# One core, an adaptive-norm block and a sparse-attention block in float32: the set-up of the first block is reordered

## The reference

```python
mod = (c @ w_ada[l] + b_ada[l])[:, None, :]            # c: (1, 1024), w_ada: (1024, 6144)
sh_m, sc_m, gt_m, sh_f, sc_f, gt_f = jnp.split(mod, 6, axis=-1)
h = rms_norm(x, g_pre_mix[l]) * (1.0 + sc_m) + sh_m
z = h @ w_in[l]
u, f, q, k, v = jnp.split(z, splits, axis=-1)
y_ssm = s5_mixer(u, lam_re, lam_im, log_dt, b_re, b_im, c_re, c_im, d_skip, w_glu)
...
x = x + gt_m * rms_norm(y, g_post_mix[l])
h = rms_norm(x, g_pre_ffn[l]) * (1.0 + sc_f) + sh_f
...
```

## Time and profile before

| | us |
|---|---|
| three runs | 3245.16, 3250.99, 3251.94 |
| median | 3250.99 |
| span of the profiled execution | 3246.9 |
| median less that span | 4.1 |
| PE busy in the span | 3019.4 (93%) |
| DVE, ACT, POOL busy in the span | 2163.2, 1251.2, 273.8 |
| first modulation matmul of the chain | 31.32 |
| tap matmuls begin | 114.04 |

### The profile page before, as it was taken

One profiled execution on the slowest core, in us unless ns is written; L12 is line 12 of the kernel. 1 busy time (PEld: TensorE's weight loads), 2 busy tenths in 40 slices (PEclk: granted clock), 3 DMA queues, 4 the chain that ended last, 5 costly groups with the idle time before them and its releaser, 6 DMA issues.

```text
span 3246.9 us, 36670 instructions
## 1 busy us (share of the span) xinstructions
PE 3019.4 (93%) x13313; PEld 2339.1 (72%) x13313; DVE 2163.2 (67%) x3880; ACT 1251.2 (39%) x2183; POOL 273.8 (8%) x287
## 2 busy tenths in 40 slices
PE   6999889799999999999999998986898799999997
PEld 2576566678888888788888875764446678888886
DVE  5562923899988667766665683997542876666567
ACT  1121333544444554433334443234543343333443
POOL 4200210110000000200000000113330010000000
PEclk9899899899999999999999997987999999999999
DMA  8323013324444874354448731111003335444864
GB/s 284 117 51 69 1 34 104 110 97 155 161 160 158 285 258 137 120 166 155 154 158 308 217 124 57 39 27 37 1 1 111 118 114 162 158 156 156 308 208 149
DMA packets 350920, 436.97 MB, mean 135 GB/s; under 512 B 35281, under 2 KB 197065, under 8 KB 350614
## 3 DMA queue, kind: packets, MB, share of 16 engines
q1 hardware_dynamic: 340954, 428.48, 40.1%
q10 hardware_dynamic: 9788, 6.16, 0.6%
HBM read 317.78 MB, written 116.50 MB: 134 GB/s over the span
## 4 chain that ended last, share of the span: by engine, by line
PE 80%; DVE 13%; ACT 3%; issue 1%; ACTq 1%; DMA 1%; POOL 0%; DVEq 0%
PE psum L1876 34%; PE psum L1333 19%; PE psum L991 4%; PE psum L3635 3%; DVE count_junk L3060 3%; PE psum L3606 3%; PE psum L1867 3%; PE psum L2680 3%; PE psum L2858 2%; PE psum L2758 1%; PE psum L2838 1%; PE psum L390 1%; DVE p L3124 1%; PE psum L2848 1%; PE psum L358 1%
## 5 line engine op out<-in xcount | busy, mean ns | idle before, releaser
L1333 PE MATMUL psum<-far_op,far_op 128*128 128x512 f32 x2772 | 629.4, 389 | 0.0
L1333 PEld LDWEIGHTS psum<-far_op,far_op 128*128 128x128 f32 x2772 | 520.2, 188 | 107.9
L1876 PE MATMUL psum<-x_b,w_near 128*128 128x512 f32 x1440 | 348.1, 391 | 3.9 <-DVE w_near L1505 3.9
L1876 PE MATMUL psum<-x_t,w_near 128*128 128x512 f32 x1440 | 337.1, 389 | 0.7 <-ACT psum L1614 0.6
L1876 PE MATMUL psum<-x_t,w_far 128*128 128x512 f32 x1440 | 336.3, 389 | 0.0
L1876 PEld LDWEIGHTS psum<-x_b,w_near 128*128 128x128 f32 x1440 | 272.0, 189 | 61.2 <-issue 4.3
L1876 PEld LDWEIGHTS psum<-x_t,w_near 128*128 128x128 f32 x1440 | 270.1, 188 | 58.0 <-ACT psum L1614 2.0
L1876 PEld LDWEIGHTS psum<-x_t,w_far 128*128 128x128 f32 x1440 | 270.2, 188 | 56.4 <-ACT u_keep L1626 0.4
L1104 DVE TENSOR_TENSOR far_op<-far_a,far_op 128x512 fp32r<-128x512 f32 x231 | 160.6, 695 | 176.2 <-ACT far_op L1097 174.7
L1097 ACT CAST far_op<-far_a 128x512 fp32r<-128x512 f32 x231 | 143.9, 623 | 315.9 <-PE psum L1333 307.7
L1876 PE MATMUL psum<-x_b,w_far 128*128 128x512 f32 x720 | 178.9, 399 | 10.1 <-DVE val_row L1746 10.1
(11 more groups left out here) (484 smaller groups left out, 5145.0 us busy)
## 6 DMA issues: line engine op xcount, KB each, us to landing
far_a<-row_ops SPq DMA_DIRECT2D x231, 256.0 KB, 2.9
row_ops<-hidden SPq DMA_DIRECT2D x99, 512.0 KB, 5.1
raw<-in_ffn_w SPq DMA_DIRECT2D x88, 512.0 KB, 4.5
col_sums<-hidden SPq DMA_DIRECT2D x66, 512.0 KB, 5.7
far_b<-col_sums SPq DMA_DIRECT2D x132, 256.0 KB, 3.2
ada_w<-in_w_ada SPq DMA_DIRECT2D x12, 2048.0 KB
raw<-in_w_up SPq DMA_DIRECT2D x44, 512.0 KB, 3.9
hidden<-in_ffn_w SPq DMA_DIRECT2D x44, 512.0 KB
```

Source lines behind the costliest of these rows:

```text
L1333: ins = t.matmul(bank(b + n), l[slot][:, rows], r[slot][:], start=(fresh and i == 0 and m == 0), stop=(i == FH - 1 and m == 2), skip_group ...
L1876: ins = t.matmul(bank(b), at[:, l, cols], x[:, k, r], start=(start and k == 0 and m == 0), stop=(k == 3 and m == 2), skip_group_check=not ...
```

## The change

Placement: `c_plain` and `e_tmp` move within the memory, `ada_b` becomes one tile of two rows of 1024, and two tiles are new: `bias_cols` [128, 4, 8] and `b_rows` [48, 2048]. Semaphore counts follow. The core of the diff, by engine.

SP queue:

```diff
             cols = slice(HALF * j, HALF * (j + 1))
-            sp.dma_start(ada_w[j % 3][:], w_ada[:, :, cols]).then_inc(ada_in[j % 3], 16)
-            sp.dma_start(ada_b[j % 3][:], a["b_ada"][:, cols]).then_inc(ada_in[j % 3], 16)
+            for k in range(0, KD, 4):
+                sp.dma_start(ada_w[j % 3][:, k:k + 4], w_ada[:, k:k + 4, cols]).then_inc(ada_in[j % 3], 16)
...
         sp.wait_ge(vec_used, 1)
-        sp.wait_ge(carry_ready, 2)
```

ACT queue, after the loads of lam_re, lam_im and log_dt:

```diff
+        act.dma_start(dskip_rows[:], a["d_skip"][0].rearrange("(g c) -> g c", c=GC)).then_inc(ssm_in, 16)
         for i, name in enumerate(("b_re", "b_im")):
             for d in range(2):
-                act.dma_start(b_raw[:, i, d, :, :],
-                              a[name][0, d].rearrange("(q e) p c -> (e p) q c", e=2)).then_inc(ssm_in, 16)
+                at_row = PAIRS * (2 * i + d)
+                act.dma_start(b_rows[at_row:at_row + PAIRS, :],
+                              a[name][0, d].rearrange("(q e) p c -> q (e p c)", e=2)).then_inc(b_c_in, 16)
         for i, name in enumerate(("c_re", "c_im")):
             for twice in range(2):
                 act.dma_start(c_rows[:, i, :, twice, :],
-                              a[name][0].rearrange("(b g) c p -> (g c) b p", b=3)).then_inc(ssm_in, 16)
-        act.dma_start(dskip_rows[:], a["d_skip"][0].rearrange("(g c) -> g c", c=GC)).then_inc(ssm_in, 16)
+                              a[name][0].rearrange("(b g) c p -> (g c) b p", b=3)).then_inc(b_c_in, 16)
...
+        for i, part in enumerate((0, 3)):
+            at_row = 2 * wide + 2 * KD * i
+            act.dma_start(vec_rows[1][at_row:at_row + 2 * KD, :],
+                          a["b_ada"][0, D * part:D * (part + 2)].rearrange("(k p) -> k p", p=P)).then_inc(vec_in, 16)
+        for i, part in enumerate((2, 5)):
+            act.dma_start(ada_b[:, i, :], a["b_ada"][:, D * part:D * (part + 1)]).then_inc(bc_in, 16)
...
-        act.wait_ge(mod_ready, 1)
         for n in range(2):
             split(n)
+        act.wait_ge(mod_ready, 1)
```

DVE (the waits on `ssm_in` go from 16 * 12 to 16 * 4):

```diff
+        def input_columns():
+
+            flat = b_raw[:].rearrange("p r d q c -> p (r d q) c")
+            for i in range(2):
+                dve.wait_ge(b_turned, i + 2)
+                steps.add(v.tensor_copy(flat[:, :, GC // 2 * i:GC // 2 * (i + 1)],
+                                        bank(6 + i, GC // 2 * 4 * PAIRS).rearrange("p (c m) -> p m c", c=GC // 2)))
+            steps.settle()
...
         steps.settle()
+        dve.sem_inc(lam_used, 1)
...
             steps.add(v.tensor_tensor(col(9), col(9), col(9), ALU.mult))
+        dve.wait_ge(c_turned, 2)
+        output_columns()
+        input_columns()
         dve.wait_ge(prm_trig, 2)
...
-            if kind % 2 and half == 1:
-                steps.add(v.scalar_tensor_tensor(mod_cols[:, kind, :], stat_c[:, 0:KD], 1.0,
-                                                 norm_cols[:, kind // 2, :], ALU.add, ALU.mult))
+            if half == 1:
+                sums = stat_c[:, 0:KD] if kind % 2 else mod_cols[:, kind, :]
+                steps.add(v.tensor_tensor(sums, sums, bias_cols[:, kind, :], ALU.add))
                 steps.settle()
-
-        dve.wait_ge(bc_in, 48)
+                if kind % 2:
+                    steps.add(v.scalar_tensor_tensor(mod_cols[:, kind, :], sums, 1.0, norm_cols[:, kind // 2, :], ALU.add, ALU.mult))
+                    steps.settle()
...
+        modulation_used(0)
+        vector_columns()
         for k in range(1, CH):
-            modulation_used(k - 1)
             complex_step(lam_b_at(k), lam_b_at(k - 1), 13, 14)
+            if k == 3:
+                dve.wait_ge(bc_in, 16 * 5)
+            modulation_used(k)
...
             elif n == 5:
+                dve.wait_ge(carry_ready, 2)
                 turns(v, steps, 0)
```

PE:

```diff
             pe.wait_ge(ada_in[j % 3], 32 * (j // 3 + 1))
-            if j == 2:
-                pe.wait_ge(vec_used, 1)
-            elif j >= 4:
+            if j >= 4:
                 pe.wait_ge(ada_used, j - 3)
+            part, half = j // 2, j % 2
+            rows = part in (2, 5)
             for k in range(KD):
-                t.matmul(bank(j % 4), c_bcast[:, k, :], ada_w[j % 3][:, k, :], start=(k == 0), stop=False)
-            t.matmul(bank(j % 4), ones_row[:], ada_b[j % 3][:], start=False, stop=True).then_inc(ada_mm, 1)
+                t_last = t.matmul(bank(j % 4), c_bcast[:, k, :], ada_w[j % 3][:, k, :], start=(k == 0), stop=(k == KD - 1 and not rows))
+            if rows:
+                pe.wait_ge(bc_in, 16 * 5)
+                t_last = t.matmul(bank(j % 4), ones_row[:], ada_b[:, part // 3, HALF * half:HALF * (half + 1)], start=False, stop=True)
+            t_last.then_inc(ada_mm, 1)
...
         pe.wait_ge(ident_in, 16)
-        pe.wait_ge(vec_in, 16 * 6)
...
-        pe.wait_ge(ssm_in, 16 * 12)
+        pe.wait_ge(ssm_in, 16 * 4)
...
         ins.then_inc(lam_turned, 1)
+        pe.wait_ge(b_c_in, 16 * 8)
+        lines = 4 * PAIRS
+        for i in range(2):
+            if i:
+                pe.wait_ge(lam_used, 2)
+            for n in range(GC // 2):
+                ins = t.transpose(bank(6 + i, lines, lines * n), b_rows[:].rearrange("r (m c) -> r c m", c=GC)[:, GC // 2 * i + n, :],
+                                  ident[0:lines, 0:lines])
+            ins.then_inc(b_turned, 1)
...
         pe.wait_ge(c_spread, 2)
-        for j in range(N_ADA - 2):
+        for j in range(2):
+            modulation(j)
+        pe.wait_ge(vec_in, 16 * 8)
+        pe.wait_ge(c_ready, 2)
+        t.transpose(bank(4, 2 * wide + 2 * KD), vec_rows[0][0:2 * wide + 2 * KD, :], ident[0:2 * wide + 2 * KD, 0:2 * wide + 2 * KD])
+        t.transpose(bank(5, 2 * wide + 4 * KD), vec_rows[1][0:2 * wide + 4 * KD, :],
+                    ident[0:2 * wide + 4 * KD, 0:2 * wide + 4 * KD]).then_inc(rows_turned, 1)
+        for j in range(2, N_ADA - 2):
             modulation(j)
```

More of the change, by code:

```diff
@@ L106, in body @@
     log_dt_rows = const("log_dt_rows", [GROUPS, 2])
+    bias_cols = const("bias_cols", [P, 4, KD])
     x_rows = place("x_rows", [P, NT, D], GR)
@@ L111, in body @@
     junk2 = place("junk2", [P, P], GR + 39 * KB + 512)
-    c_plain = place("c_plain", [P, 2, PAIRS, GC], GR + 36 * KB)
+    c_plain = place("c_plain", [P, 2, PAIRS, GC], RR + 19 * KB)
     ada_w = [place(f"ada_w{i}", [P, KD, HALF], at) for i, at in enumerate((XR, XR + 16 * KB, GR + 64 * KB))]
     c_bcast = place("c_bcast", [P, KD, P], RR + 40 * KB)
-    ada_b = [place(f"ada_b{i}", [1, HALF], at) for i, at in enumerate((XR + 56 * KB, XR + 58 * KB, GR + 80 * KB))]
+    ada_b = place("ada_b", [1, 2, D], GR + 80 * KB)
+    b_rows = place("b_rows", [4 * PAIRS, P * GC], XR + 32 * KB)
     vec_rows = [place(f"vec_rows{i}", [P, P], RR + 512 * i) for i in range(2)]
@@ L121, in body @@
     w_tmp = place("w_tmp", [P, 2, 4, PAIRS, GC], RR + 34 * KB)
-    e_tmp = place("e_tmp", [P, 4, PAIRS, GC], RR + 4 * KB)
+    e_tmp = place("e_tmp", [P, 4, PAIRS, GC], RR + 16 * KB)
     c_pad = place("c_pad", [P, 2, PAIRS, 2, GC], XR + 60 * KB)
@@ L153, in body @@
     lam_turned, c_turned, c_ready = sem("lam_turned"), sem("c_turned"), sem("c_ready")
+    b_turned, lam_used = lam_turned, dt_spread
     prm_angle, prm_trig, prm_lam = (sem(n) for n in ("prm_angle", "prm_trig", "prm_lam"))
     lam_b_ready, win_turned, win_ready, k_mm, k_ready = (sem(n) for n in ("lam_b_ready", "win_turned", "win_ready", "k_mm", "k_ready"))
-    carry_ready, k_shift_in, k_low, k_in_dram, toep_in = (sem(n) for n in ("carry_ready", "k_shift_in", "k_low", "k_in_dram", "toep_in"))
+    carry_ready, k_shift_in, k_in_dram, toep_in = (sem(n) for n in ("carry_ready", "k_shift_in", "k_in_dram", "toep_in"))
+    b_c_in, K_SHIFT_0 = k_shift_in, 16 * 8
     x_sq, x_var, x_std, x_scaled, x_turned, h_ready = (sem(n) for n in ("x_sq", "x_var", "x_std", "x_scaled", "x_turned", "h_ready"))
@@ L743, in body @@
     out_first, out_raw, out_s31, out_s42, wt_in, OUT_0 = ada_in[0], ada_in[1], x_in, toep_in, ada_in[2], 16 * NT
-    out_t13, T13_0, out_t42, T42_0 = ssm_in, 16 * 12, k_in_dram, 16 * 15
+    out_t13, T13_0, out_t42, T42_0 = ssm_in, 16 * 4, k_in_dram, 16 * 15
     s_sums, S_SUMS_0, wt_sums, WT_SUMS_0 = y_mm, 6, x_turned, 2 * KD
-    ops_in, OPS_IN_0 = (small_in, ident_in, bc_in, vec_in, k_shift_in, fw_in), (16, 16, 48, 96, 16, 80)
+    ops_in, OPS_IN_0 = (small_in, ident_in, bc_in, vec_in, k_shift_in, fw_in), (16, 16, 80, 128, K_SHIFT_0 + 16, 80)
     f_hi, f_lo, f_mm, F_0 = win_hi, z_ready, win_mm, len(win_units)
@@ L3337, in _ @@
         v.tensor_copy(c_bcast[:], c_cols[:].unsqueeze(2).to_broadcast([P, KD, P])).then_inc(c_spread, 1)
-        dve.wait_ge(ssm_in, 16 * 12)
+        dve.wait_ge(ssm_in, 16 * 4)
         v.tensor_copy(lam_rows[:, 2, :].rearrange("r (e p) -> r e p", e=2),
                       log_dt_rows[:].unsqueeze(2).to_broadcast([GROUPS, 2, STATE])).then_inc(dt_spread, 1)
[L3342 to L3351, removed]
-        steps.add(v.memset(c_pad[:], 0.0))
```

(65 more changed lines are left out.)

2 lines of the change are left out of this document (1 added, 1 removed).

## The result

The changed kernel takes 3228.6 us (median of 4 runs, 3215.8 to 3230.7), the kernel before 3251.15 (median of 4, 3245.2 to 3251.9). The ratio of the two is 0.9929, with a 95% interval of 0.9913 to 0.9945: 22.5 us less, where 20.4 was forecast. The profiled executions show less, spans of 3246.9 and 3228.6, 18.3 us. The time of the profiled execution after is 3230.67, so 2.1 us lie around the span; the 4.1 taken in the prediction held some 2 us by which that execution was simply faster than the median.

What follows compares the result with a forecast made beforehand. PE's chain, started by the ACT queue's loads, was taken as the bound. 13.3 + 8.4 - 0.6 - 0.7 = 20.4 us off 3250.99 gave 3230.6; the range was 3223 to 3242.

Steps and rivals of the forecast that it cites:

- the 4.1 taken in the prediction: Whole kernel: the median was taken to stand 4.1 us above the profiled execution's span.
- PE and not DVE is the chain: Set-up: PE sets the end; DVE's lam_b_ready at 89.5, 4 us ahead of PE at 93.6.
- PE's start: Set-up: PE begins modulation 0 at 18.0 (bounds 15.9 and 20.2) instead of 31.32, 13.3 us earlier.
- the landing of b and c: Set-up loads: landed at 11.3, or 14.8 with c at 88 ns a run; 12.6 us taken.
- Rival 2: Set-up loads: c lands at 20 to 22, PE starts about 26; gain 12.4, time 3239; chance 0.12.
- The bias: PE, first ten modulations: eight lose their bias pair of 1.05 each, 8.4 us less.
- Vector rows: PE between modulations 1 and 2: two transposes of the vector rows added, cost 0.6 us.
- late slice: PE ahead of modulation 2: wait for w_ada's third slice, 0 to 1.6 us, 0.7 taken.
- DVE: DVE's set-up chain: waits for c at 17.1, step 0 at 25.9, lam_b_ready at 89.5; additions cost nothing.
- 4: Set-up loads: c takes 2.1 at 22 ns per run, PE starts at 14.5; gain 23.9, time 3227; chance 0.09.
- 5: Set-up loads: b's 12-row loads run on one DMA engine, landing at 44; gain -11, time 3262; chance 0.04.
- 1: Set-up: DVE becomes the bound, price 4.6, gain 15.8, time 3235; chance 0.14.

Runs made afterwards that it cites:

- e4: Changed kernel with w_ada's first load issued only when b and c have landed; 3231.7 us, median of 5 runs.
- e8: Changed kernel with a bias pair in all 12 modulations (for eight, the row added is not the bias); 3247.0 us, ratio to before 0.9991.
- e5: Changed kernel with w_ada's slices 1 and 2 issued only when b and c have landed, slice 0 at once; 3234.0 us, median of 10 runs.
- e7: Changed kernel with b loaded in runs of 64 B straight into its layout, its transposes and copies gone; 3239.1 us, ratio to before 0.9966.
- e1: Changed kernel with each slice of w_ada in one load instead of two; 3231.1 us, ratio to before 0.9941.
- e2: Changed kernel with each slice of w_ada in four loads instead of two; 3232.6 us, ratio to before 0.9942.
- e12_before_hold: Kernel before with w_ada's slices 1 and 2 issued only when all state-space parameters have landed; 3232.0 us, 1 run.

## Why the prediction was right, and where it was not

- *PE and not DVE is the chain, and a us ahead of the taps is a us at the end.* Right: chain and margin are as read, 2.2 us where 4 were expected.
- *PE's start, 13.3 us earlier.* Wrong by 8.8: it was 4.5. The failed term is the landing of b and c, 11.3 to 14.8 forecast, 23.4 measured, and it failed in two places. b was priced by its bytes, 2.2 us, to be through by 4.8; its last row ended at 12.0. Alone, in e4, it was through at 7.1, so the long rows cost more than their bytes without w_ada too, and the step from there to 12.0 is w_ada beside them; why the rows are so slow stays open. c was taken near the average pace of 51 ns. That average mixed two paces of before: 93 ns a run beside w_ada, and 10 ns once it was through (2,152 runs from 22.2 to 23.6 us). c now had w_ada beside it to the end and went at 101 ns, over even the 88 of the upper bound. Rival 2 (landing at 20 to 22, PE at 26) is what happened, and its cause, c at 88 ns behind b's rows, is near to what was found. The rest of the term was too dear: 16 transposes in 2.0 us, 0.125 each, not 3.9.
- *The bias, 8.4 us.* Right on PE: 9.0 in e8. But its whole worth was 12.4 us of set-up, since the taps ran 3.4 us faster behind modulations without pairs. No term of the sum had that: the taps' 18.19 and modulation 10's 9.46 were carried over as fixed.
- *Vector rows 0.6, late slice 0.7.* 0.2, and no wait for w_ada in the chain: slice 2 was there at 31.6, ahead of the 34.3 of the forecast, and PE wanted it only at 42.4. x, taken as issued from 10 us on, was issued from 15.9, behind c.
- *DVE.* The copies of c and b took 3.6 us (26.89 to 30.46), as forecast (2.5 + 1.1). From step 0 to `lam_b_ready` 62.9 us against the forecast's 63.6, POOL keeping its phase; the additions cost nothing. ACT's Sin, forecast at about 17, came at 28.4, since the issues ahead of it were held as well; DVE, busy with c and b until 30.46, didn't notice, and would have had to wait if c had come when forecast.
- *Rivals.* 4, c at 22 ns a run, would hold only with w_ada out of the way (22 ns in e5 behind slice 0). It drew on the rule of the Trainium skill ("DMA: Bandwidth & Descriptors", Queues, rings and completion order) that a DMA engine takes several descriptors of one queue before it turns to the other. The equal counts, 953 and 952, fit turns of any one length, so the rule is neither shown nor refuted here; what fell is the conclusion that c would come sooner by it. 5 falls with the landing itself, 23.4 and not 44, and with e4. 1 was close and came true only in e7, by another way than named.

So the total came out by errors of opposite sign, and that is luck: 8.8 us too much for PE's start, against 1.6 too little for the ten modulations, 1.1 too much taken off for rows and slice, and 3.5 too little behind the taps' start. With 17.7 us in the set-up, the profile falls short of the forecast's 20.4; that the medians differ by 22.5 is within the scatter of the part behind, and e1 and e2, with the same set-up, came out at 19 and 18.

## What to carry to other kernels

When small loads and a large stream share the DMA engines, count runs on both sides. Here every small run cost a turn of the large stream, some 0.1 us on each engine, whether it was 64 or 256 B, until one side was out; an average pace taken over both states fits neither. And hold back what isn't needed soon: with w_ada held they came 13 us sooner, but the gain is only kept if nothing else, here x, takes the freed place. An engine that both issues loads and computes delays its computing when its queue is full, here ACT's Sin by 7.2 us. And what is cut ahead of a stretch of small matmuls can change the clock at which that stretch runs, here by 3.4 us of 27.6.

## What was not expected of the hardware

- Two DMA queues of one core moved equal numbers of runs while both had some (953 and 952, 2,066 and 2,066), although a run of the one had 8 or 32 times the bytes of the other's.
- PE's time at the 1.2 GHz level after the taps began took one of three values: 13.7, 17.1 and 20.5 us. It was 20.5 in all three kernels with bias pairs in each of modulations 7 to 9: before, e8_pairs and e12_before_hold.
- Back to back, a transpose of 48 rows with a stride of 64 B came every 0.125 us (2.00 / 16), half of a 128-row one's 0.245.
- The part behind the set-up, the same work in all fourteen kernels, took 3081.8 to 3099.3 us, at mean granted clocks of 0.966 to 0.961: a scatter of 0.6% that a single execution can't see through.
